# Another placement of the prepared pieces of the next differential head among the steps of the running one

## What is computed

```python
def _diff_attn(q, k, v, lam_vecs, gain, lam_init, pos, valid):
    q = _rope(_to_heads(q, 2 * DA_HEADS), pos).reshape(b, DA_HEADS, 2, l, DA_DQK)
    k = _rope(_to_heads(k, 2 * DA_HEADS), pos).reshape(b, DA_HEADS, 2, l, DA_DQK)
    ...
    def block(args):
        qi, bi = args
        s = jnp.einsum('bhcqd,bhckd->bhcqk', qi, k) * scale
        ...
        p = jax.nn.softmax(jnp.where(mask, s, NEG), axis=-1)
        w = p[:, :, 0] - lam * p[:, :, 1]
        return jnp.einsum('bhqk,bhkv->bhqv', w, v)
```

## Time and profile before

| | us |
|---|---|
| median of 3 runs | 3672.7 (3671.28 to 3696.09) |
| the profiled execution | 3665.27 |
| its span | 3663.3 |
| differential heads 0 to 2, layer 0 (514.8 to 710.4) | 195.6 |
| differential heads 0 to 2, layer 1 (2331.8 to 2526.3) | 194.5 |

### The profile page before, as it was taken

One profiled execution on the slowest core, in us unless ns is written; L12 is line 12 of the kernel. 1 busy time (PEld: TensorE's weight loads), 2 busy tenths in 40 slices (PEclk: granted clock), 3 DMA queues, 4 the chain that ended last, 5 costly groups with the idle time before them and its releaser, 6 DMA issues.

```text
span 3663.3 us, 49829 instructions
## 1 busy us (share of the span) xinstructions
PE 3243.4 (89%) x16426; PEld 2071.7 (57%) x16426; DVE 1645.5 (45%) x2639; ACT 788.3 (22%) x1853; POOL 167.1 (5%) x239
## 2 busy tenths in 40 slices
PE   7999788898895899999689998888988949999996
PEld 5666456666553555555356664566764425555553
DVE  5777524555324233233367774356543242232234
ACT  3222224432110011111132221244321101111113
POOL 1300000000000000000200000000000000000002
PEclk8999898888796899999889999988878969999997
DMA  5910100001002799999710000000010038999996
GB/s 167 254 30 11 42 12 7 8 7 58 5 35 119 311 408 408 415 409 409 301 34 25 23 23 19 12 7 7 7 58 11 35 155 338 411 410 409 415 407 245
DMA packets 136556, 592.53 MB, mean 162 GB/s; under 512 B 13000, under 2 KB 47816, under 8 KB 119016
## 3 DMA queue, kind: packets, MB, share of 16 engines
q1 hardware_dynamic: 105688, 491.41, 34.0%
q0 software_dynamic: 20400, 72.69, 6.0%
q10 hardware_dynamic: 10336, 26.75, 1.9%
HBM read 524.55 MB, written 66.26 MB: 161 GB/s over the span
## 4 chain that ended last, share of the span: by engine, by line
PE 82%; DVE 8%; issue 5%; ACT 2%; DMA 1%; DVEq 0%; POOL 0%; ACTq 0%; POOLq 0%; SPq 0%
PE ps L1073 7%; PE ps L1268 7%; PE ps L1376 7%; PE ps L1445 7%; PE ps L1486 7%; PE ps L1451 6%; PE ps L1476 6%; PE ps L1114 6%; PE ps L1207 4%; PE ps L1339 3%; PE ps L1503 3%; PE ps L1169 3%; PE ps L1194 2%; PE ps L1285 2%; DVE negmax L1755 1%
## 5 line engine op out<-in xcount | busy, mean ns | idle before, releaser
L1114 PE MATMUL ps<-arena 128*128 128x260 f32 x1024 | 294.4, 421 | 7.6 <-DVE arena L1701 7.4
L1755 DVE TENSOR_REDUCE negmax<-ps 16x1 f32<-16x16 f32 (+8 forms) x216 | 151.7, 705 | 264.3 <-PE ps L1174 263.4
L1073 PE MATMUL ps<-arena 128*128 128x512 f32 (+1 forms) x768 | 257.5, 494 | 7.3 <-ACTq L571 3.5
L1376 PE MATMUL ps<-arena 128*128 128x512 f32 (+1 forms) x576 | 252.3, 596 | 0.0
L1268 PE MATMUL ps<-arena 128*128 128x256 f32 (+1 forms) x1152 | 251.8, 380 | 0.0
L792 ACT ACTIVATE arena<-ps,negmax 16x16 f32<-16x16 f32 (+8 forms) x216 | 150.8, 699 | 469.1 <-DVE negmax L1755 465.4
L1445 PE MATMUL ps<-arena 128*128 128x512 f32 x544 | 248.1, 610 | 2.0 <-DVE arena L2233 2.0
L1486 PE MATMUL ps<-arena 128*64 128x256 f32 x2176 | 242.3, 381 | 0.0
L1451 PE MATMUL ps<-arena 128*128 128x256 f32 x1088 | 240.4, 379 | 0.0
L1476 PE MATMUL ps<-arena 128*128 128x512 f32 x544 | 239.1, 592 | 0.0
L1451 PEld LDWEIGHTS ps<-arena 128*128 128x128 f32 x1088 | 206.7, 190 | 42.6 <-issue 16.3
(11 more groups left out here) (339 smaller groups left out, 4331.3 us busy)
## 6 DMA issues: line engine op xcount, KB each, us to landing
arena<-w SPq DMA_DIRECT2D x204, 2048.0 KB, 13.6
xg<-arena POOLq DMA_DIRECT2D x51, 512.0 KB, 12.3
xg<-arena ACTq DMA_DIRECT2D x34, 512.0 KB, 7.5
arena<-w_in SPq DMA_DIRECT2D x16, 1024.0 KB, 5.5
xg<-arena ACTq DMA_DIRECT2D x68, 128.0 KB, 9.3
arena<-w_in SPq DMA_DIRECT2D x16, 512.0 KB, 4.0
arena<-w_out SPq DMA_DIRECT2D x2, 4096.0 KB, 12.7
u_rows<-arena SPq DMA_DIRECT2D x16, 512.0 KB, 2.6
```

The costliest lines, as they stand in the source:

```text
L1073: mm = pe.matmul(dst[0:hi - lo, a:b], w[:, k, lo:hi], uT[:, k, a:b], start=(k == 0), stop=(k == KD - 1))
L1114: mm = pe.matmul(out, w_qk[b][:, k, :], uT[:, k, lo:hi], start=(k == 0), stop=(k == KD - 1), skip_group_check=True)
L1376: mm = pe.matmul(ps[0:r, 3 * (j % 2) + half, :], mT[:, j % 2, k, 0:r], w_o[:, k, half * 512:half * 512 + 512], start=(k == 0), stop=(k == ...
L1755: v.tensor_reduce(negmax[0:r, at:at + 1], flat[0:r, side:side + wide_], AX.X, ALU.max, negate=True)\
```

## The change

Only the placement table of the differential pieces and the pieces issued ahead of the first head change. No instruction is added or removed. Replication pieces c to f and rotation pieces b move to later points in steps 0 to 6, the projection pieces shift with them, and `d0` of the head after next is issued at point 53, in step 8, and no longer at point 1 of the next head.

```diff
 PLAN_DA = {
-    0: [["b1@6"], ["d0@2"], ["a2.0@1"], ["e0@6"], ["f0@2"], ["a2.1@1"]],
-    1: [["c1@6"], [], ["a2.2@1"], ["d1@6"], [], ["e1@6", "a2.3@1"]],
-    2: [["g@4"], ["f1@6"], ["b2@2"], [], [], ["c2@6"]],
-    3: [["a3.0@2"], ["d2@6"], [], ["e2@6", "a3.1@2"], [], ["f2@6", "a3.2@2"]],
-    4: [[], ["a3.3@2"], [], [], ["b3@6"], []],
-    5: [["o@6"], ["a0.0@2+"], ["c3@6"], [], ["d3@6", "a0.1@2+"], []],
-    6: [["e3@6"], ["a0.2@2+"], ["f3@6"], [], ["h@6", "a0.3@2+"], []],
+    0: [["a2.0@1"], ["e0@2"], [], ["f0@6"], ["b1@2"], ["a2.1@1"]],
+    1: [[], ["a2.2@1"], ["c1@6"], [], ["d1@2"], ["a2.3@1"]],
+    2: [["g@4"], ["e1@6"], [], ["f1@2"], ["b2@6"], []],
+    3: [["a3.0@2"], [], ["c2@6"], ["a3.1@2"], ["d2@6"], []],
+    4: [["e2@6"], ["a3.2@2"], ["f2@6"], ["a3.3@2"], [], ["b3@6"]],
+    5: [["a0.0@2+"], ["o@6"], [], ["c3@6"], ["a0.1@2+"], ["d3@6"]],
+    6: [[], ["e3@6", "a0.2@2+"], [], ["f3@6"], ["a0.3@2+"], ["h@6"]],
     7: [[], ["b0@6+"], [], ["a1.0@6+"], [], ["a1.1@6+"]],
-    8: [[], ["a1.2@6+"], [], ["a1.3@6+"], ["c0@2+"], []]}
+    8: [[], ["a1.2@6+"], [], ["a1.3@6+"], ["c0@2+"], ["d0@6+"]]}
@@ pieces_at
-    out = [(1, "c0@2")] if slot == 0 else []
+    out = [(1, "c0@2"), (1, "d0@6")] if slot == 0 else []
```

## The result

| | before | after |
|---|---|---|
| median of 11 runs each, us | 3673.94 (3667.06 to 3696.09) | 3648.40 (3638.10 to 3661.61) |
| ratio, 95% interval | | 0.9925 (0.9905 to 0.9944) |
| profiled execution, us | 3665.27 | 3647.10 |
| its span | 3663.3 | 3645.2 |
| heads 0 to 2, layer 0 and layer 1 | 195.6, 194.5 | 185.0, 184.9 |

The changed kernel is 0.75% faster by the ratio; the medians are 25.5 us apart. Heads 0 to 3 of both layers account for 15.1 of the 18.2; the other 3.1 lie in code that is the same.

A forecast was written before the change was run, and what follows sets the result against it. PE, busy 80% in heads 0 to 2, was held by waits on other engines and 105 us at half clock. Waits +3.8 and shrinkage -5 gave -1.2 on the 3672.7 median: 3671.5 us, range 3653 to 3689.

The forecast's parts named there:

- 10.65 common to all heads, 37.9 per layer against 36.0: New PE waits in heads 0 to 2 replace the eight largest old rows: +3.8 us over both layers.
- c2: At point 20, waits 1.0 us per head: 3.35 of DVE chain against 2.4 of PE work; before, 2.6.
- f3: Replication piece at point 39, expected to wait 1.0 us in each head.
- a1.0: Projection piece after b0, waited 1.85 us before; expected 1.2, as DVE's join has run on.
- e3: At point 37, waits 2.5 us behind d3's copy, itself behind the exponential of 912 columns; no wait before.
- The correction of -5: Over all new waits: they shrink at half clock, up to -7.6 us, of which -5 was taken.
- I leave the 105 us as they are: Heads 0 to 2 of both layers: time at half clock stays 105 us, costing about 39.
- Rival 1: Steps 1 to 4: the clock holds, half of 105 us returns to full clock, 19 us gained: 3652; chance 0.22.
- rival 2: Waits clustered at c3, e3, f3, b0, a1.0: clock falls more often, +19 us: 3691; chance 0.16.
- Rival 3: From d2 on, pieces follow their bank's last product by two points, its copy by one: 3671.5; chance 0.55.
- Rival 4: Steps 1 and 2 do not get shorter, chain 4.9 us, +13 over six heads: 3685; chance 0.07.
- d0: Moved from point 1 to 53 at no cost; 0.4 us of PE work changes sides.

The follow-up runs named there:

- changed again: The changed kernel measured once more, nothing altered: 3654.28 us, ratio 0.9941 to the kernel before.
- late only: The kernel before with only steps 5 and 6 at their new points: 3689.56 us, ratio 1.0037.
- d0 back: The changed kernel with d0 back in step 0 of the next head, at point 0 behind a2.0: 3648.00 us, ratio 0.9941.
- h late: The early only kernel with h moved from point 40 to 41: 3650.22 us, ratio 0.9935.
- early only: The changed kernel with steps 5 and 6 as before, except a0.0 and o in their new order: 3641.98 us, ratio 0.9902.
- h ahead of the maximum: The e3 earlier kernel with f3 at point 37, h at 39 and a0.1 ahead of d3: 3613.99 us, ratio 0.9848.
- e3 earlier: The changed kernel with d3 moved from point 35 to 34, e3 from 37 to 36, a0.1 behind them: 3618.51 us, ratio 0.9852.
- d2 covered: The e3 earlier kernel with a3.2 moved from point 25 to 22, ahead of d2: 3616.68 us, ratio 0.9830.
- all waits: The h ahead of the maximum kernel with a3.2 ahead of d2 at point 22 and a3.3 at 25: 3620.93 us, ratio 0.9862.

## Why the prediction was wrong

I forecast 3671.5 us (range 3653 to 3689); it is 3648.4, 4.6 us below the range. Within 1% was right by the ratio of 0.9925.

**The waits.** The prediction's step "10.65 common to all heads, 37.9 per layer against 36.0" failed: the sum over both layers fell by 18.2 us and did not rise by 3.8. Term by term, per layer, forecast and measured in layer 0:

| | forecast | measured |
|---|---|---|
| c2 | 3.0 | 0 |
| f3 | 3.0 | 0.8 |
| a1.0, two heads | 2.4 | 0.4 |
| c3 | 5.6 | 4.6 |
| e3 | 7.5 | 6.8 |
| c1, f2 | 1.2 | 0.4 |
| d2 | 3.0 | 3.0 |
| b3 | 3.9 | 3.6 |
| b0, and a0.0 in head 2 | 4.8 | 4.4 |
| b2 | 2.2 | 2.3 |
| o and d3 in head 2 | 1.4 | 1.4 |
| e2, b1, scores, transposes | 0 | 2.2 |

Every wait that I named stands or fell at the place named, so the mechanism was right, but for c2, which does not wait at all. Three terms were mis-sized, 7.2 us per layer, 14.4 in all, of the 22.0 between +3.8 and -18.2; the rest are small errors that nearly all go the same way. My terms hold at full clock; what half clock took from the measured ones is told below.

- *c2.* I had 3.35 us of chain against 2.4 of PE work. Counted from the end of b2 (590.58), the split was done after 2.7 and the PE's own work took 2.7. The chain was too long by 0.6: I had put 0.5 ahead of the rotation, where DVE began 0.16 after b2; rotation, maximum and split took 2.5 on DVE, where I had 2.07 and 0.71; and my own three terms give 3.28, not 3.35. The work was too short by 0.3: outputs took 0.79 and not 0.4, and a3.0 1.12.
- *f3.* It waited 0.27 in all six heads, and in all six the PE was at half clock just before:

```profile
618.80:621.24 2.44, 2.44 (x9) 1.69 (x8) 0.00 (x0) 0.75 (x2) 0.00 (x0) 0.50 0.03 7
```

```profile
621.51 0.56 PE L1132 MATMUL ps<-rounded,gamma_r 128*128 128x260 f32 x1 [0.27 <-ACT rounded L766]
```

  In the four kernels with this order (changed, changed again, late only, d0 back) f3 waits 0.27 wherever the 0.8 us before its wait are at half clock, and more the higher the mean clock there: 0.45 at 0.72, 0.58 at 0.80. Drawn on to full clock that is some 0.8, an estimate, against my 1.0. At half clock the PE's scores of 912 columns ahead of f3 took 1.11 us, at full clock 0.57; ACT's copy took 0.38 at either, and the wait shrinks by the difference. That e3 came late itself does not shorten f3's wait by the rows: the copy that f3 waits for stands behind one of transposes that the PE issues after e3.
- *a1.0.* While the PE stands at b0 for 1.54, DVE's join runs on. Behind that wait a1.0 has 0.58 left at full clock (all four heads of h late) and 0 at half clock (all four of d0 back). Taking b0's wait away brought a1.0's 1.85 back. I had written "as DVE's join has run on" and allowed 0.65 for it; it was 1.27, and half clock took most of the rest here.

**The correction of -5** for waits that shrink at half clock was right in kind and about right in size. In the changed kernel f3 lost some 3 us by it over six heads, a1.0 1.7 over four, and e3 1.0 over six (2.43 at full clock, 2.17 at half): about 6, an estimate, of the gap of 22.0. The other 16 are wrong sizes: c2 6.0, a1.0 2.5 and many small ones.

**Head 3** the sum put at nothing. It took 5.1 us more over both layers, at a lower clock.

**The clock.** "I leave the 105 us as they are" came true by number, and by luck. Without head 3 the mean clock is 0.87 and 0.86; with head 3, half clock went from 122 to 128 us (118 in the repeat). But this is the difference of two large effects. Count each stretch at half clock where it begins. Up to the wait of c3 (steps 0 to 4) there were 44 us before, 10 and 7 in the two profiles of the changed kernel, 10 and 3 in those of early only, and 58 in late only. From c3 on in heads 0 to 2 there were 61 before, 89 and 85, 65 and 85, and 75; in head 3 14 before, 27 and 27, 24 and 21, and 27. So the early moves keep the first steps at full clock, and part of that comes back later in the head. In time the early moves gave -20 us of waits and -6 to -9 of clock, the late ones +2 and +4 to +11; these ranges come from two profiles of either kernel. Rival 1 (the clock holds) and rival 2 (it falls more often) both happened, one in steps 0 to 4 and one in steps 5 to 8, and I had given them as alternatives for the whole.

**Rival 1** gave 3652, near to what was measured, from a cause that is not the one here: half clock did not fall over the whole of the changed kernel's heads. **Rival 2's** cluster of c3, e3, b0 is real. In the changed kernel every fall of the clock in heads 0 to 2 comes within 2.3 us of the end of a wait of 0.8 to 2.4 us, mostly c3, e3, b0 and d2, and none of these waits is longer than 2.4. Over all fourteen profiles 149 of 156 falls come as near to a wait of 0.8 us or more, or within it, though only a third of the time lies as near to such a wait. Late only has the waits of before (78.2 and 77.2) in other places, and pays 35 us more at half clock. The Trainium skill (TensorE: Matmul & The Clock Gate, A second HAM failure mode: psum-queue depth-cycling) tells of a PE that is briefly idle between groups and swings between its two clocks. The trace agrees with 17 falls in six heads and no wait over 2.4 us; no run here tests whether going round the PSUM banks is what matters. **Rival 3** was the right account of the places. **Rival 4** (steps 1 and 2 do not get shorter) did not happen: steps 1 and 2 of head 1 took 3.5 and 4.0 us, where I had counted on 3.8 and 3.9, and rival 4 on 4.9. **d0** at no cost was right.

**What would show it.** Right: no wait at e1 and f1, e3 at 2.2 to 2.4 with the exponential of 912 columns ahead, b0 behind L1688, b3 at 1.21, mean clock between 0.82 and 0.91. Wrong: c2 at 0 and not 1, and a total of 30.0 and 29.4 us, at and under the bound of 30 that I had set for "wrong".

**The measurement.** The traces account for 15 to 17 us in heads 0 to 3 (changed, and changed again). Of the 25.5 us 7.4 lie in which execution was profiled and 3.1 in later code; what they are is not shown. I had added the change to the median, which is right, but profiled executions differ from their medians by up to 11 us (h ahead of the maximum), as much as the effects in question.

**What stays open.** Which waits bring a long stretch at half clock and which a short one. In head 2 the clock falls in all kernels once more between 34 and 46 us after the head's start. It stays down for 20 to 24 us in the changed kernel, and for 3 to 10 with e3 earlier or d2 covered; but h ahead of the maximum and all waits, which have e3 as early, are back at 17 to 24. h one point later brought 20 to 30 us of half clock with a smaller sum of waits, while the kernel with e3 earlier has h at that same point and little half clock. That the sum of the waits does not set it is shown; a rule by which one could have said it beforehand isn't.

## What to carry to other kernels

Write a sum of new waits as a timeline, not as a list: a wait gives the other engines time, so the next wait can shrink by it (a1.0: 1.85 alone, 0.58 behind b0's 1.54), and removing one hands it on (b3 to f2's copy, b0 to a1.0). Where waits of one to two microseconds stand close together, price them twice, as idle time and at 0.37 us for each us at half clock; here the one wait of e3, in six heads, went with 10 us of idle time and 12 to 15 of clock. How much half clock a wait will bring could not be said beforehand. Split a table's edit into its halves before judging it: this one held a gain of some 33 us and a loss of 12 to 14.

## What the runs showed of the hardware that I had not expected

- The length of heads 0 to 3 is a constant plus the PE's waits plus 0.37 us for each us at half clock, within 3.5 us of some 450, over fourteen profiles with 70 to 157 us at half clock.
- Waits of the PE for other engines shrink while it is at half clock: c3 behind DVE waits 1.53 us at full clock and 0.75 at half (d2 covered), a1.0 behind b0 0.58 and 0, f3 up to 0.58 and 0.27.
- The clock's cost outlives the heads in which the waits stand: head 3, whose instructions never changed, took 49.5 us at a mean clock of 0.93 and 52.0 at 0.87.
- With one piece moved by one point (h, 40 to 41) the median was 14 us higher in a run of 3640, though the PE waited less in all. In the profiles 3 to 8 us of it lie in heads 0 to 3 and 6 to 11 in later code that is the same, which differs by up to 13 us over the fourteen profiles anyhow; for that part the cause isn't shown.
